# One layer of a gated hybrid encoder on one core: rotated tiles with other places, values as the last plain tile, and zeros of the low keys by DMA

## What is computed

```python
h = rms_norm(x, g_pre)
a_b, a_c, a_x, a_z, b_q, b_k, b_v, b_z, m_q, m_z, gate_logits = split(h @ w_in)
ya = short_gated_conv(a_b, a_c, a_x, w_conv) * silu(a_z)
q, k = partial_rope(b_q, pos), partial_rope(b_k, pos)   # 8 query heads, 2 key heads of 64
yb = window_attention_with_sink(q, k, b_v, attn_sink) * silu(b_z)   # blocks of 128, +-128
ym = memory_cross_attention(m_q, mk, mv) * silu(m_z)    # mk, mv from rms_norm(mem) @ w_mem_kv
gates = sigmoid(gate_logits)
out = (gates[0] * (ya @ w_up_a) + gates[1] * (yb @ w_up_b) + gates[2] * (ym @ w_up_m)) @ w_out
return x + rms_norm(out, g_post)
```

## Time and profile before

| | |
|---|---|
| median of three runs | 950.99 us (948.83 to 951.58) |
| profiled execution, its own time | 951.5 us |
| its span in the trace | 949.7 us |
| PE busy (matmul / weight load) | 918.8 us (97%) / 770.2 us (81%) |
| DVE, ACT, POOL busy | 623.2, 421.9, 386.9 us (66%, 44%, 41%) |
| DMA | 122.33 MB, mean 129 GB/s, engines busy 39% |

### The profile page before, as it was taken

One profiled execution on the slowest core, in us unless ns is written; L12 is line 12 of the kernel. 1 busy time (PEld: TensorE's weight loads), 2 busy tenths in 40 slices (PEclk: granted clock), 3 DMA queues, 4 the chain that ended last, 5 costly groups with the idle time before them and its releaser, 6 DMA issues. The chain is left out here.

```text
span 949.7 us, 12513 instructions
## 1 busy us (share of the span) xinstructions
PE 918.8 (97%) x4360; PEld 770.2 (81%) x4360; DVE 623.2 (66%) x1053; ACT 421.9 (44%) x802; POOL 386.9 (41%) x266
## 2 busy tenths in 40 slices
PE   5999889999999999999999999999999999999997
PEld 4787668888888888888888888888888888888885
DVE  5799947656565656655577178988797367764443
ACT  7434356444445456555561534343444544432211
POOL 2576834444444444444443844444443636210000
PEclk9999999999999999999999999999999999999999
DMA  7133735343424243534344412222222974642222
GB/s 280 66 89 102 183 122 169 101 155 104 147 100 147 100 137 100 174 107 155 107 135 167 150 56 78 80 85 82 84 78 71 334 253 153 213 156 67 89 89 88
DMA packets 79629, 122.33 MB, mean 129 GB/s; under 512 B 6992, under 2 KB 38864, under 8 KB 79568
## 3 DMA queue, kind: packets, MB, share of 16 engines
q1 hardware_dynamic: 79568, 121.55, 39.2%
HBM read 88.49 MB, written 33.03 MB: 128 GB/s over the span
## 5 line engine op out<-in xcount | busy, mean ns | idle before, releaser
L637 POOL TENSOR_TENSOR ring<-spots,ring 128x512 fp32r<-128x512 f32 x218 | 308.4, 1418 | 392.1 <-ACT ring L1041 379.3
L713 PE MATMUL pm<-hc,ring 128*128 128x512 f32 x728 | 288.0, 396 | 3.5 <-POOL ring L637 3.5
L715 PE MATMUL pm<-hc,ring 128*128 128x512 f32 x728 | 285.1, 392 | 0.0
L714 PE MATMUL pm<-hc,ring 128*128 128x512 f32 x728 | 284.7, 391 | 0.0
L1041 ACT ACTIVATE ring<-spots 128x512 fp32r<-128x512 f32 x218 | 136.2, 628 | 255.2 <-PE pm L715 184.3
L713 PEld LDWEIGHTS pm<-hc,ring 128*128 128x128 f32 x728 | 137.5, 189 | 31.1 <-issue 4.3
L715 PEld LDWEIGHTS pm<-hc,ring 128*128 128x128 f32 x728 | 137.2, 188 | 29.3
L714 PEld LDWEIGHTS pm<-hc,ring 128*128 128x128 f32 x728 | 137.6, 189 | 27.0
L1265 ACT ACTIVATE area<-area 128x1024 f32<-128x1024 f32 x24 | 25.4, 1060 | 59.4 <-DMA area<-raw_d 59.4
L991 PE MATMUL pm<-hc,ring 128*128 128x512 f32 x128 | 49.9, 390 | 0.0
L992 PE MATMUL pm<-hc,ring 128*128 128x512 f32 x128 | 49.8, 389 | 0.0
(11 more groups left out here) (208 smaller groups left out, 1630.1 us busy)
## 6 DMA issues: line engine op xcount, KB each, us to landing
spots<-in_w SPq DMA_DIRECT2D x116, 256.0 KB, 3.2
raw_d<-area SPq DMA_DIRECT2D x72, 256.0 KB, 2.0
area<-raw_d SPq DMA_DIRECT2D x24, 512.0 KB, 3.5
area<-in_x SPq DMA_DIRECT2D x16, 512.0 KB, 5.0
spots<-in_wup SPq DMA_DIRECT2D x24, 256.0 KB, 3.8
q_d<-area_r SPq DMA_DIRECT2D x16, 256.0 KB, 4.2
area_r<-q_d SPq DMA_DIRECT2D x8, 512.0 KB, 3.9
area<-raw_d SPq DMA_DIRECT2D x16, 256.0 KB, 3.6
```

The costliest lines, as they stand in the source:

```text
L637: nc.gpsimd.tensor_tensor(ring[:, n % RING, 1, :], operand(n), ring[:, n % RING, 0, :].bitcast(F32), ALU.subtract).then_inc(lo_made, 1)
L713: pe.matmul(bank, hi, moving_hi(k), start=(k == 0), stop=False)
L714: pe.matmul(bank, hi, moving_lo(k), start=False, stop=False)
L715: mm = pe.matmul(bank, lo, moving_hi(k), start=False, stop=(k == HC - 1))
```

## The change

- The values tile becomes the last plain tile (tile 5, bank sa[0:2]) and the last query tile takes its place (tile 4, bank pm[1]). So P6 and P7 of pair 3 wait for `times_cos(4)` instead of the copy of the values, `times_cos(4)` no longer waits for the last plain tile, and the values are copied by ACT after pair 2's last slot, into the place of `v_pair` (which also held T2's sums: so the copy waits for T2's low parts).
- Rotated tiles: five entries in `ROTATED`, of which the first four alternate as before and the fifth is a place of its own. `times_cos(4)` waits for no store; `rope_high(4)` on ACT waits for the stores of tile 2 instead, for the high part's buffer.
- DVE's order: swap and cosine of tile 2 go ahead of the T4 sums; the low half of T1 goes from between `times_cos(3)` and `rotate(3)` to after `add_p6` of pair 3; `make_values` goes from P7 of pair 3 to P3 of pair 3, where `clear_keys` was.
- ACT's order: the high parts of T1 and weight part 14 come before `rope_high(2)`, `rope_high(3)` goes to P2 and `rope_high(4)` to P7 of pair 3. POOL's order: T1's low parts and weight part 14 come before `rope_low(2)`, part 16 before `rope_low(3)`, part 17 before `rope_low(4)`.
- SP's order: the stores of tiles 2, 3, 4 go to P1, P6, P4 of pair 3 (after the weight loads that are issued there).
- Low keys: `kl_d` gets both halves. The zeros come from 32 rows of the sine table that are zero, by four DRAM-to-DRAM transfers of 128 KB issued early on SP; the low keys' store is two DMAs; `clear_keys` goes, and `load_block` takes the low keys with one DMA of 384 KB in place of two of 96 KB. The wait for all stored rotations moves from DVE to SP.
- `take_c11` of pair 3 waits for three combinations on POOL instead of four.

```diff
-TILES = [(T_K, T_Q), (T_Q + 1, T_Q + 2), (T_V, T_Q + 3)]
+TILES = [(T_K, T_Q), (T_Q + 1, T_Q + 2), (T_Q + 3, T_V)]
 for first, count in ((T_ZB, AC), (T_GA, KC), (T_GB, KC), (T_ZM, AC), (T_GM, KC), (T_MQ, AC)):
...
 X0, B11F, B21F, B12F, B22F, T3F = 0, 8192, 10240, 12288, 0, 2048
-COS0, SIN0, SWAP0, ROT1, QHI0, ROT0, VR0, VP0 = 4096, 5120, 6144, 7168, 0, 2048, 3072, 12288
+COS0, SIN0, SWAP0, QHI0, VR0, VP0 = 4096, 5120, 6144, 0, 12288, 12288
+ROTATED = (7168, 2048, 7168, 2048, 3072)
 QS0, KWH0, KWL0, PR0, PTH0, PTL0, OS0, OO0 = 0, 1024, 1792, 2560, 4096, 5632, 7168, 7680
...
-ROPES = [(0, None), (1, 0), (2, 1), (3, 2), (5, 3)]
-V_TILE = 4
+ROPES = [(0, None), (1, 0), (2, 1), (3, 2), (4, 3)]
+V_TILE = 5
...
         kh_d = dram("kh_d", (P, 2, SEQ))
-        kl_d = dram("kl_d", (P, SEQ))
+        kl_d = dram("kl_d", (P, 2, SEQ))
         ob_d = dram("ob_d", (AC, P, SEQ))
...
         rope_high_at = [f32r(QHI0 + n * SEQ, SEQ) for n in range(2)]
-        rope_low_at = [f32r(at, SEQ) for at in (ROT1, ROT0)]
+        rope_low_at = [f32r(at, SEQ) for at in ROTATED]
         memx = f32(MX0, 2 * D).rearrange("p (b d) -> p b d", b=2)
...
         def rotated(j):
-            return f32((ROT1, ROT0)[j % 2], SEQ)
+            return f32(ROTATED[j], SEQ)
...
         raw_stored = [sem(f"raw_stored{j}") for j in range(4)]
-        v_turned, v_made, kz_made = sem("v_turned"), sem("v_made"), sem("kz_made")
+        v_turned, v_made, zero_stored = sem("v_turned"), sem("v_made"), sem("zero_stored")
         q_landed, kh_landed, kl_landed = sem("q_landed"), sem("kh_landed"), sem("kl_landed")
...
         def wait_stored(eng, j):
-            eng.wait_ge(rope_stored[j], 16 * (5 if ROPES[j][1] is None else 4))
+            eng.wait_ge(rope_stored[j], 16 * (6 if ROPES[j][1] is None else 4))
...
                 c = ROPES[j][1]
-                high, low, done = rope_high_at[j % 2].bitcast(F32), rope_low_at[j % 2].bitcast(F32), rope_stored[j]
+                high, low, done = rope_high_at[j % 2].bitcast(F32), rope_low_at[j].bitcast(F32), rope_stored[j]
                 sp.wait_ge(rope_lo, j + 1)
...
                         sp.dma_start(kh_d[other, g, :], high[own, :]).then_inc(done, 16)
+                        sp.dma_start(kl_d[own, g, :], low[own, :]).then_inc(done, 16)
                     else:
...
                                      low[own, :].rearrange("p (b q) -> p b q", b=NB)).then_inc(done, 16)
-                if c is None:
-                    sp.dma_start(kl_d, low).then_inc(done, 16)
...
                 load_spot(j, 1)
+
+            for g in range(2):
+                for part in range(2):
+                    row = (1 - g) * HEAD + part * HEAD // 2
+                    sp.dma_start(kl_d[row:row + HEAD // 2, g, :], sin[ROT:ROT + HEAD // 2, :]).then_inc(zero_stored, 16)
             sp.wait_ge(x_turned, 2 * KC)
...
             store_rope(1)
-            store_rope(2)
...
                 if i == 0:
-                    sp.wait_ge(kz_made, 1)
+                    for j in range(len(ROPES)):
+                        wait_stored(sp, j)
+                    sp.wait_ge(zero_stored, 16 * 4)
                 else:
...
                 sp.dma_start(kwin_hi_f32, kh_d[:, :, first:first + WIN]).then_inc(kh_landed, 16)
-                for g in range(2):
-                    own = slice(g * HEAD, (g + 1) * HEAD)
-                    sp.dma_start(kwin_lo_f32[own, g, :], kl_d[own, first:first + WIN]).then_inc(kl_landed, 16)
+                sp.dma_start(kwin_lo_f32, kl_d[:, :, first:first + WIN]).then_inc(kl_landed, 16)
...
                     load_spot(A11, p + 1)
+                    if p == P_DIRECT:
+                        store_rope(2)
                     if p == P_ATT:
...
                     load_spot(A21, p + 1)
-                    if p == P_DIRECT:
-                        store_rope(3)
                     store_block(p - 1, "next P2")
...
                     if p == P_DIRECT:
-                        store_rope(4)
+                        store_rope(3)
                     if 0 <= gr < ATT_GROUPS - 1 and gr % 2 == 1:
...
                     store_block(p - 1, "next P7")
+                elif name == "P4":
+                    if p == P_DIRECT:
+                        store_rope(4)
+                    if p == P_LAST:
+                        load_gate(0)
                 elif name == "P5":
...
                         load_mq(p + 1 - P_CONV)
-                elif name == "P4" and p == P_LAST:
-                    load_gate(0)
                 store_block(p, name)
...
                 pool.wait_ge(rope_hi, j + 1)
-                nc.gpsimd.tensor_tensor(rope_low_at[j % 2], rotated(j), rope_high_at[j % 2].bitcast(F32),
+                nc.gpsimd.tensor_tensor(rope_low_at[j], rotated(j), rope_high_at[j % 2].bitcast(F32),
                                         ALU.subtract).then_inc(rope_lo, 1)
...
             low_part(13)
-            rope_low(2)
-            low_part(14)
             for j in (0, 2):
                 low_of_combination(T1, j)
+            low_part(14)
+            rope_low(2)
             low_part(15)
+            low_part(16)
             rope_low(3)
-            low_part(16)
+            low_part(17)
             rope_low(4)
-            for n in range(17, NS + 3):
+            for n in range(18, NS + 3):
                 low_part(n)
...
                 else:
-                    pe.wait_ge(v_copied, 1)
+                    pe.wait_ge(cos_made, 5)
                 if p == P_DIRECT and idx in SPLITS:
...
                     pe.wait_ge(kh_landed, 16 * (i + 1))
-                    pe.wait_ge(kl_landed, 32 * (i + 1))
+                    pe.wait_ge(kl_landed, 16 * (i + 1))
                 for h in range(GROUP):
...
                         pe.wait_ge(v_made, 2)
-                        pe.wait_ge(cos_made, len(ROPES))
                     else:
...
                     act.wait_ge(comb_hi, 2 * HC)
+                elif j == 4:
+                    wait_stored(act, 2)
                 nc.scalar.activation(rope_high_at[j % 2], rotated(j), ACT.Copy).then_inc(rope_hi, 1)
...
             high_part(13)
-            wait_slot(act, 2, "A12")
-            nc.scalar.copy(v_raw, tile_bank(V_TILE)).then_inc(v_copied, 1)
-            rope_high(2)
             high_of_combination(T1)
             high_part(14)
+            rope_high(2)
             high_part(15)
-            rope_high(3)
+            wait_slot(act, 2, "A22")
+            act.wait_ge(comb_pool, 4)
+            act.wait_ge(comb_dve, 4)
+            nc.scalar.copy(v_raw, tile_bank(V_TILE)).then_inc(v_copied, 1)
...
                     if p == P_DIRECT:
-                        rope_high(4)
+                        rope_high(3)
                     if p - 1 in SILU:
...
                 elif name == "P7":
+                    if p == P_DIRECT:
+                        rope_high(4)
                     if 0 <= gr < ATT_GROUPS:
...
                 if p == P_DIRECT:
-                    dve.wait_ge(comb_pool, 2 * len(SPLITS))
+                    dve.wait_ge(comb_pool, 2 * len(SPLITS) - 2)
                 elif P_SPILL < p <= P_CONV:
...
                 dve.wait_ge(rope_landed, 32)
-                if j >= 2:
+                if 2 <= j < 4:
                     wait_stored(dve, j - 2)
...
             rotate(1)
+            swap_rows(2)
+            times_cos(2)
             for j in range(HC):
...
             low_of_combination(T2)
-            swap_rows(2)
-            times_cos(2)
             low_of_combination(T4)
...
             times_cos(3)
-            low_of_combination(T1)
             rotate(3)
...
                 dve.wait_ge(comb_pool, 2 * len(SPLITS))
+                dve.wait_ge(v_turned, 2)
                 for half in range(2):
-                    dve.wait_ge(v_turned, half + 1)
                     bank = (sa[:, 2, :], pv[:, :])[half].rearrange("p (b d) -> p b d", b=4)
...
                     ins.then_inc(v_made, 1)
-
-            def clear_keys():
-                for j in range(len(ROPES)):
-                    wait_stored(dve, j)
-                nc.vector.memset(kwin_lo_f32[HEAD:P, 0, :], 0.0)
-                nc.vector.memset(kwin_lo_f32[0:HEAD, 1, :], 0.0).then_inc(kz_made, 1)
...
                     add_p6(p)
+                    if p == P_DIRECT:
+                        low_of_combination(T1)
                     if p - 1 in SILU:
...
                     add_p7(p)
-                    if p == P_SPILL:
-                        make_values()
                     if p == P_CONV - 1:
...
                     if p == P_DIRECT:
-                        clear_keys()
+                        make_values()
                     if p == P_CONV - 2:
```

## The result

The changed kernel takes 953.49 us (median of 11 runs, 952.80 to 954.99) beside 951.04 for the kernel before in the same rounds: ratio 1.0022, 95% interval 1.0013 to 1.0031. That is 2.1 us more by the ratio (2.45 between the two medians). The interval lies clear of no change, but the difference is under the 0.3% that the prediction took as its bound for calling a kernel slower. The forecast was 951.2, its range 948.8 to 954.8. The profiled execution took 953.27, with a span of 951.5 and a mean granted clock of 0.993.

A forecast was written before the change was run, and what follows sets the result against it. PE was taken as bound by nearly unbroken matmuls, idle mainly between plain tiles and Strassen pairs. Delays before P1 were paid back by vanished later gaps; scores at 128.1 instead of 127.98 gave +0.2 us: 951.2, range 948.8 to 954.8.

The forecast's parts named there:

- Steps 1 and 2: Tile 2 ahead on DVE: PE's 1.59 us wait goes; 2.65 idle plus 2.2 collisions delay P1 of pair 3 to 96.5.
- Step 3: P1 to P7 of pair 3: slow clock adds 1.6 us, hidden by the wait for tile 4's cosine; P7 ends 109.8.
- Step 4: Gaps before P4 and P5 of pair 3 go; pair 4's P2 ends 123.8 against 123.9, paying back the loss.
- Step 5: Last rotation: rope_high(4) done 111.4, rope_low(4) 113.8, stores start 113.9, the last lands 120.7.
- Step 6: First attention load: memset wait becomes a wait for tile 4's store; raw-store path ready 120.6; load leaves 120.7, before 120.87.
- Step 7: First attention load with one 384 KB low-key transfer: 7.4 us from issue to scores, which start 128.1; later blocks hide it.
- Step 8: Values made on DVE from 122.8 to 125.7, hidden with 2.4 us to spare; zero transfers nearly free, -0.1 to +0.3 us.
- A: Rival: first attention load leaves early, 3.2 us sooner; shorter gap without slow clock saves another 1.5; 947.4 us; chance 0.12.
- B: Rival: DVE's chain later still, times_cos(4) ending after 105.5, passed one for one to the scores; +2 to +3.5, 954.5; chance 0.16.
- C: Rival: clock stays low through P6 and P7, each product costing 2.4 us more; about 956 us; chance 0.04.
- D: Rival: larger key loads show in all eight blocks, 0.64 us of DMA each; up to 954 us; chance 0.03.

The follow-up runs named there:

- e6_own_place: Changed kernel with rotated tile 2 in a place of its own, so its cosine waits for no store; ratio to the kernel before 1.0013.
- e8_t1_back: Changed kernel with T1's high parts back behind rope_high(2) on ACT and its splits behind rope_low(2) on POOL; ratio to the kernel before 0.9982.
- e3_load_early: Changed kernel with rope_high(4) ahead of weight part 19 and the first attention load right behind tile 4's stores; ratio to the kernel before 1.0006.
- e1_order_back: Changed kernel with swap and cosine of tile 2 back behind the T4 sums and T2's low half on DVE; ratio to the kernel before 0.9978.
- e2_rope4_early: Changed kernel with only rope_high(4) moved ahead of weight part 19 on ACT; ratio to the kernel before 1.0011.
- e13_order_early: Changed kernel with the edits of e1_order_back and e10_early together; 946.94 us, ratio to the kernel before 0.9947.
- e4_more_keys: Changed kernel with another 256 KB, read by nothing, in each of eight attention loads, scores waiting for it; ratio to the kernel before 1.0045.
- e12_both: Changed kernel with the moves of e8_t1_back and e10_early together; ratio to the kernel before 0.9978.
- e10_early: Changed kernel with rope_high(3) and (4) ahead of their weight parts, first attention load behind tile 4's stores, values at P7; ratio to kernel before 0.9962.

## Why the prediction was right, and where its steps were off

The range held and the shape of the stage came as laid out, but the forecast said next to no change (0.2 us) and the ratio says 2.1 us more, clear of its interval. Part of the agreement is luck, and it is named below.

**Steps 1 and 2** hold in their result: tile 5 without a wait, DVE idle 2.31 (2.65 forecast), cosine of tile 3 ending 96.2 (96.4), gap 5.31 (5.4), P1 at 96.30 (96.5). Two things in them were luck. The store's landing at 75.0 was put together as 69.1 and 5.9; in fact the last store left at 70.27 and landed at most 4.7 later. And the sum took the idle time and the collisions as two costs that add. In the changed kernel's trace both are there, but e6_own_place shows that without the idle time 2.07 of its 2.31 us come back as collisions in the T4 sums, and e8_t1_back that T1's early place alone holds some 3 us. The idle time was not a cost of its own.

This is where the Trainium skill bears on the case. It states (SBUF — State Buffer, section "SBUF: two separate sides") that DVE with two SBUF inputs and GpSimd reading SBUF take an exclusive lock for a whole instruction, and that the later one blocks. The traces agree: an addition of 0.68 grows to 1.60 to 1.78 beside a split, while the cosine product at 95.03, which reads PSUM, keeps its 1.21 beside POOL's operation from 94.87 to 97.23.

**Step 3** has the one term that was mis-sized: the slow clock behind P1's gap, put at 1.6 from the one drop in the earlier trace rows and called hidden by the wait for the cosine of tile 4. P1 and P2 took from 96.30 to 104.60, 8.30 against 5.44 at full clock: 2.9, with 0.50 granted until about 102.2. That is 1.3 more than forecast, and it was not hidden: the cosine ended at 103.07, so P6 started 1.5 later than it had to. (In e8_t1_back, where the clock was low for 3.4 us, it was hidden.) P7 ended at 110.94 instead of 109.8, and another 0.25 is the time from the last matmul's turn to its result, after which ACT starts at 111.19.

**Step 4** holds: no gap before P4 or P5, and one of 0.55 before P3 (under 0.7). Its last sentence, that the loss is paid back by P2 of pair 4, does not: PE was done there at 125.5, not 123.8, and 1.6 later than in the kernel before.

**Step 5** ran as laid out, each station 1.4 late: `rope_high(4)` behind part 19 ended 112.77 (111.4), first store 115.28 (113.9).

**Step 6** found the right holder. The last store starts at 117.55 and lands 4.7 later, 122.25; the load leaves at 122.41 (120.7). The raw store left at 120.93 and the weight load behind it at 121.36, so that path was 0.5 us ahead of the store and cost nothing more; without it, in e3_load_early, SP waited for the store alone.

**Step 7** came out in size: 7.40 from issue to scores, 7.4 forecast. That is luck in part: the same three loads took 6.88 in e1_order_back, 7.21 in e3_load_early, 8.68 in e2_rope4_early and 9.08 in e13_order_early. The fit of the Trainium skill that the step sets beside it (DMA: Bandwidth & Descriptors, "Anatomy of one DMA — SWDGE (gpsimd) path") is stated for a DMA that GpSimd issues; here SP issues them. The new load of 384 KB of low keys landed 6.2 us after its issue, against the 2.9 worked out from that fit.

**Step 8** holds: values made from 123.79 to 126.8, 3 us before the scores. The zeros cost nothing that the trace shows: behind them, ahead of the changed work, PE starts its tile at 68.94, where it was 68.97.

**The rivals.** A did not occur: the store held the load. B's mechanism did not either, since `times_cos(4)` ended at 103.1, far from 105.5; but the delay that B priced, passed one for one through P6, P7, the store and the load, did occur with the slow clock as its source. C fell: the clock was 1.00 from 103 until the gap before the scores. D fell by e4_more_keys; its price was also worked out wrongly, since 0.64 us in each of seven later blocks would give 955.7 and not 954, outside the range. On the profiled execution the forecast was 951.7; with the 1.7 by which the scores came later than forecast that makes 953.4, and 953.27 was measured. So the miss is 1.4 from step 3, its term and its 0.25 less the 0.2 by which P1 was early, carried on by step 5, and 0.3 from the store's landing in step 6. The medians add 0.7: the profiled execution lay 0.5 above its median before, and 0.2 below it after.

**What is settled and what is open.** Shown: with the rest of the change in place the order on DVE costs about 4.2 us, and the rest without it brings about 2.1; moving T1's work back instead of DVE's order recovers as much, so the loss belongs to the two moves together. Shown: with the order back, no gap stands before P1. Argued, not shown: how much of the 4.2 is the gap and how much the slow clock behind it; e6_own_place gives 1.2 for a difference of clock and little else. The 2.1 us of gain are not split among the other moves by any run. Why the same gap is followed by more or less slow clock from one kernel to another stays open.

## What to carry to other kernels

A wait that is removed at one end of a queue moves everything behind it against the other engines' work: before moving an operation ahead, lay the next ten operations of both engines side by side, and ask what they meet. Where a gap of TensorE is the result, price the slow clock behind it as a range (0 to 3 us here), not as one number, and ask whether the next wait hides it. And follow a gain to the next thing that holds the path: with the store holding the load, moving P1 forward another 3 us (e12_both after e10_early) brought only a longer gap before the scores.

## What the runs showed of the hardware

The clock after a gap varies more than expected. Behind gaps before P1 of 5.31, 4.93 and 5.24 us the granted clock stood at 1.2 GHz for about 5.9, 2.8 and 3.4 us (from the slices). Part of the difference is where the fall lies: in the changed kernel the clock fell 0.9 us before P1 started, in e6_own_place 0.6 before, in e10_early just behind its start, and from the fall on it was low for 6.8, 3.4 and 3.4 us. A gap of 2.17 (e8_t1_back) was followed by slow clock, one of 2.14 at the same place (e12_both) and one of 3.58 (e1_order_back) by none. What this is worth behind the scores shows between the first and the last scores, where the work is the same: 347.7 to 347.8 us in the three traces without slow clock there, 349.1 to 350.4 in the others, so 1.4 to 2.7 us. The last column of the table also holds what differs behind the last scores, 472.4 to 473.4 us, for which the runs give no cause.

The Trainium skill (TensorE: Matmul & The Clock Gate, "Part 1: The HAM clock gate") says that activity releases the throttle and that the count of slow matmuls differs from run to run. The traces agree as far as they go: each low stretch ended while matmuls ran, and P1's was 5.9, 2.8 or 3.4 us long behind nearly the same gap. They show it in mid-kernel as well. They are of different kernels, one execution each.

The same three loads took 6.9 to 9.1 us from first issue to scores in the eight kernels in which the scores waited for them, while weight loads were in flight, so a landing in such a stage is known to about one microsecond either way.
